# Value tiles between the first modulation's blocks, feature tiles made quarter by quarter, two modulation blocks in fp32

## The chip, the cores and the metric

The kernel runs on one core of a Trainium2 chip. The metric is the device time of one execution in microseconds. The reference is one step of a diffusion backbone with one layer: 128 context tokens and 512 latent tokens (640 together), width 2048, 8 neighbourhood heads and 8 latent-attention heads, a feed-forward width of 5632, all in float32.

## The reference, cut to what matters

```python
mod = silu(cond) @ w_mod + b_mod          # (2, 6*2048): a row for context, one for latent tokens
sh1, sc1, g1, sh2, sc2, g2 = split(mod, 6)
h = x * (1 + sc1) + sh1                   # needs the first two of the six parts, for all 2048 features
z = h @ w_in                              # q, k, v of the neighbourhood heads, then the latent projections
o = concat(neighbourhood_attention(...), latent_attention(...)) @ w_o
x = layernorm(alpha * x + g1 * o)
x = layernorm(alpha * x + g2 * swiglu(x * (1 + sc2) + sh2))
```

The change touches the first three steps: the shift and scale of the first modulation, h, and the columns of w_in that give the values v of the neighbourhood heads.

## The kernel before, in words

Matrix products run on TensorE in a split form: a float32 operand is cut into a high part (a copy rounded to fp32r, made by ScalarE) and a low part (the difference, made by VectorE), and a product is high x high, high x low and low x high. So every weight block of 128 x 1024 floats (512 KB) goes through DMA, one ScalarE instruction (`mod_split` or `split`, lines 917 and 904), one VectorE instruction (lines 1394 and 1343) and then TensorE. The counters `hi_ready`, `lo_ready` and `used` tell the next engine how many blocks, over all kinds, are through; each engine's program is written out in a fixed order.

The first modulation has 64 blocks, 8 for each of 8 units of 512 columns (0 to 3 shift, 4 to 7 scale), taken in order. They land in a ring of eight buffers `mraw`, loaded by the SP queue as soon as the low part of the block eight back is made. High and low parts have four buffers each. TensorE (`mod_block`) multiplies the two conditioning rows, as a stationary operand of 4 columns, with 512 moving columns, four matmuls a block; the result of a unit is 4 x 512 in one PSUM bank. ScalarE copies it to `modrow` (line 928), and TensorE turns the rows to columns (`turn_rows`, line 2020, four small fp32 matmuls) in bank 6. When all eight units are turned, VectorE adds the bias for all features at once (`mod1`, lines 1409 and 1410).

Then h is made, 16 feature tiles of 128 x 640: VectorE scales and shifts x into `pb` (line 1419, two instructions), ScalarE copies it to the high part `hh` (line 945), VectorE subtracts to get the low part `hl` (line 1424). Tiles 0 to 5 come with value block 0, then two with each block up to 5. x is loaded behind the last modulation block, alternating with the first four value blocks.

The value stage has 16 weight blocks: two halves of 512 output columns, 8 blocks of two feature tiles each. A block serves five token tiles of 128 (`tok_block`, lines 1942 to 1944), in PSUM banks 0, 1, 2, 3 and 7; a tile is six matmuls of 512 columns. The weights' parts have two buffers, so the split of block b + 2 waits for block b. Beside these blocks VectorE computes 16 blocks of the other modulation parts by multiply-add over the weights (`gemv`, line 1371), as many in each value block as `V_MODS` says: one in blocks 4 to 11, two in 12 to 15. Their partial sums are added on TensorE (`row_sums`, lines 1953 and 1954, fp32). Then come the neighbourhood blocks, the attention, the latent projections, w_o and the feed-forward part. POOL prepares bias tables from the moment the last unit is turned (line 709) and loads further constants into x's place when all of h is made (line 719).

Of the kernel before, what the change touches and what calls it, by code (L numbers as in the profile page):

```python
# [14 lines left out]
P = 128  # L15
# [41 lines left out]
V_MODS = [0] * 4 + [1] * 8 + [2] * 4  # L57
# [12 lines left out]

def stream_order():

    order = [("w", n) for n in range(B_V + 2)]
    m = 0
    for b in range(16):
# [23 lines left out]
POS = {x: p for p, x in enumerate(ORDER)}  # L99
MOD_SEQ = [x for k, x in ORDER if k == "m"]  # L100
# [13 lines left out]
def stream_row(p):  # L114

    kind, n = ORDER[p]
# [53 lines left out]
def build(nc, wstream, xT, xtok, cond, bmod, rpb, kcT, vc, ckvcT, krcT, lncol, lnrow, latg, bcol, rope, cap, ident, sel,  # L170
# [14 lines left out]
    with ctx:  # L185
# [37 lines left out]
        nq.close()  # L223
        qh = sb("qh", [P, T], f32r, att)
        kh = sb("kh", [P, KEYS], f32r, att)
        vh = sb("vh", [P, 6, P], f32, att)
        pb = sb("pb", [P, 3, T], f32, att)
        PT = sb("PT", [P, 5, LAT], f32, att)
# [7 lines left out]
        mraw = sb("mraw", [P, 8, 1024], f32, s0)  # L236
        mhi = sb("mhi", [P, 4, 1024], f32r, s0)
        mlo = sb("mlo", [P, 4, 1024], f32r, s0)
        modrow = sb("modrow", [4, 2, 512], f32, s0)
        selt = sb("selt", [5, 2 + 2 * P], f32, s0)  # L240
# [74 lines left out]
        xstage = acc[:, :].rearrange("p (k t) -> p k t", k=KD)  # L315
        vall = acc[:, 0:6 * NH * P].rearrange("p (k d) -> p k d", k=6)
# [184 lines left out]
        def slot_of(kind, n):  # L501
            return POS[(kind, n)] % 4

        def in_count(kind, n):

            return 16 * ((POS[(kind, n)] - B_V) // 4 + 1)
# [66 lines left out]
        MOD_BANKS = [7, 5]  # L573
# [23 lines left out]
        def _(sp):  # L597
            for n in range(8):
                sp.dma_start(mraw[:, n, :], wstream[n]).then_inc(mod_loaded[n], 16)
            with sp.Fori(1, B_V // 8) as i:  # L600
                for s in range(8):

                    sp.wait_ge(lo_ready, i * 8 + (s - 7))
                    sp.dma_start(mraw[:, s, :], wstream[i * 8 + s]).then_inc(mod_loaded[s], 16)

            for g in range(8):
                sp.dma_start(xstage[:, 2 * g:2 * g + 2, :], xT[:, 2 * g:2 * g + 2, :]).then_inc(x_in[g], 16)
                if g < 4:
                    sp.dma_start(raw[:, g, :], wstream[stream_row(B_V + g)]).then_inc(loaded[g], 16)

            def stream_load(p):

                sp.wait_ge(lo_ready, p - 3)
                sp.dma_start(raw[:, p % 4, :], wstream[stream_row(p)]).then_inc(loaded[p % 4], 16)

            for p in range(B_V + 4, len(ORDER)):
                stream_load(p)

            def gu_load(i, jj):
                for q in range(4):  # L620
                    if i is None and jj == 0:
                        sp.wait_ge(lo_ready, max(p for p in range(len(ORDER)) if p % 4 == q) + 1)
# [55 lines left out]
        def _(pool):  # L678
# [12 lines left out]

            for n in range(3):
                pool.memset(unit[:, n:n + 1], float(n == 1)).then_inc(unit_set, 1)
            pool.memset(PT[:, 1, 3 * P:4 * P], 0.0).then_inc(unit_set, 1)
# [10 lines left out]
            pool.wait_ge(mod1_psum, 8)  # L705
            for a in range(NH):
# [184 lines left out]
        def _(act):  # L891
# [6 lines left out]
            def split(i, n):  # L898

                act.wait_ge(loaded[slot_of("w", n)], at(i, 32, in_count("w", n)))  # L900
                if i is not None or n >= B_V + 2:

                    act.wait_ge(used, at(i, 4, n - 1))
# [7 lines left out]
            def mod_split(i, n):  # L911

                act.wait_ge(mod_loaded[n % 8], at(i, 32, 16 * (n // 8 + 1)))
                if i is not None or n >= 4:

                    act.wait_ge(used, at(i, 16, n - 3))
                nc.scalar.activation(mhi[:, n % 4, :], mraw[:, n % 8, :], ACT.Copy).then_inc(hi_ready, 1)

            def mod_pair(i, p):

                for b in range(16):
                    c = 2 * p + b // 8
                    if b % 8 == 7:

                        act.wait_ge(used, at(i, 16, 8 * c + 8))
                        if i is not None or c >= 2:
                            act.wait_ge(mod1_psum, at(i, 2, c - 1))
                        nc.scalar.activation(modrow[:, b // 8, :], ps[MOD_BANKS[b // 8]][0:4, :],
                                             ACT.Copy).then_inc(modrow_ready, 1)
                    n = 16 * p + b + 4  # L930
                    if i is not None or n < B_V:
                        mod_split(i, n)

            for n in range(4):
                mod_split(None, n)
            mod_pair(None, 0)
            with act.Fori(1, 3) as i:
                mod_pair(i, 0)
            mod_pair(None, 3)
            split(None, B_V)  # L940
# [6 lines left out]
            for b in range(16):  # L947
                if b < 6:
                    for k in (range(6) if b == 0 else range(2 * b + 4, 2 * b + 6)):
                        h_part(k)  # L950
                        if b == 0 and k == 1:
                            split(None, B_V + 1)
# [383 lines left out]
        def _(dve):  # L1336
# [3 lines left out]
            def split(i, n):  # L1340

                dve.wait_ge(hi_ready, at(i, 4, n + 1))
# [49 lines left out]
            def mod_split(i, n):  # L1392
                dve.wait_ge(hi_ready, at(i, 16, n + 1))
                V.tensor_tensor(mlo[:, n % 4, :], mraw[:, n % 8, :], mhi[:, n % 4, :].bitcast(f32),
                                ALU.subtract).then_inc(lo_ready, 1)

            for n in range(16):
                mod_split(None, n)
            with dve.Fori(1, 4) as i:
                for n in range(16):  # L1400
                    mod_split(i, n)
            split(None, B_V)

            dve.wait_ge(mod1_psum, 8)
            dve.wait_ge(consts_in, 16 * CONSTS)
# [3 lines left out]
            V.tensor_tensor(mod1[:, 0:KD, :], psum1[:, 0:KD, :], bc[:, 0:KD, :], ALU.add)  # L1409
            own.link(V.scalar_tensor_tensor(out=mod1[:, KD:2 * KD, :], in0=psum1[:, KD:2 * KD, :], scalar=1.0,  # L1410
                                            in1=bc[:, KD:2 * KD, :], op0=ALU.add, op1=ALU.add))

            def h_part(k):
                dve.wait_ge(x_in[k // 2], 16)
                if k >= 3:
# [10 lines left out]
            for b in range(16):  # L1426
                if b < 6:
                    ks = list(range(6) if b == 0 else range(2 * b + 4, 2 * b + 6))
                    if b == 0:
                        h_part(0)  # L1430
                    for k in ks:
                        if k + 1 < KD:
                            h_part(k + 1)
                        h_rest(k)
                        if b == 0 and k == 1:
                            split(None, B_V + 1)
# [500 lines left out]
        def _(pe):  # L1937
# [60 lines left out]
            def mod_block(i, n, b, chunk_free, bank, hi, lo):  # L1998

                pe.wait_ge(lo_ready, at(i, 16, n + 1))  # L2000
                if b == 0 and chunk_free is not None:

                    pe.wait_ge(modrow_ready, chunk_free)
                for kk in range(2):
                    w = slice(kk * 512, (kk + 1) * 512)
                    mm(ps[bank][0:4, :], condw[:, 2 * b + kk, :], hi[:, w], start=(b == 0 and kk == 0), stop=False)
                    ins = mm(ps[bank][0:4, :], condw[:, 2 * b + kk, :], lo[:, w], start=False, stop=(b == 7 and kk == 1))
# [5 lines left out]
            def turn_rows(i, c):  # L2013
                if i is None:
                    pe.wait_ge(consts_in, 16 * CONSTS)

                pe.wait_ge(modrow_ready, at(i, 2, c + 1))
                for j in range(4):
                    o = at(i, 16, 8 * c + 2 * j)
                    ins = mm(ps[6][:, bass.ds(o, 2)], modrow[:, c % 2, j * P:(j + 1) * P], selt[0:4, 0:2],  # L2020
                             start=True, stop=True)
                ins.then_inc(mod1_psum, 1)

            def mod_pair(i):
                for b in range(16):
                    c = b // 8
                    mod_block(i, b, b % 8, None if i is None else i * 2 + c - 1, MOD_BANKS[c],
                              mhi[:, b % 4, :], mlo[:, b % 4, :])
                    if b % 8 == 2 and (i is not None or c):
                        turn_rows(i, c - 1)  # L2030

            mod_pair(None)
            with pe.Fori(1, 4) as i:
                mod_pair(i)
            turn_rows(None, 7)

            for c in range(2):
                for b in range(8):
# [574 lines left out]
```

## Time and profile before

| | us |
|---|---|
| median of 3 runs | 2899.25 |
| lowest, highest | 2896.92, 2899.45 |
| profiled execution | 2901.91 |
| its span | 2900.4 |
| TensorE busy in it | 2817.4 (97%) |
| VectorE busy | 1890.2 (65%) |
| ScalarE busy | 1043.8 (36%) |
| DMA, mean rate | 131 GB/s |

The span runs from the first to the last recorded instruction of the profiled execution. Busy shares are averages over the whole span; the first 220 us, to which the change belongs, look otherwise and are shown by stretches further down. PE is TensorE, DVE VectorE, ACT ScalarE, PEld the weight loads of TensorE.

### The profile page before, as it was taken

What the parts mean: (1) busy time and instruction counts of PE and PEld (TensorE: products, weight loads), DVE (VectorE), ACT (ScalarE), POOL (GpSimd) and SP (SyncE); (2) the same over time, 40 slices, a digit from 0 to 9 for tenths busy, and PEclk for the clock granted to TensorE, in tenths of its full rate; (3) what the DMA queues carried; (4) which work ended last, traced back from release to release, by engine and by line L of the source; (5) the groups of instructions that cost most, each with busy time, mean ns of one, the idle gap of its engine ahead of it and who ended that gap; (6) DMA issues with size and microseconds to landing.
All of it is one profiled execution on the core that took longest, in us unless ns stands there. A gap on an engine that the chain in (4) does not pass through costs nothing.

```text
span 2900.4 us, 42090 instructions
## 1 busy us (share of the span) xinstructions
PE 2817.4 (97%) x15844; PEld 2497.6 (86%) x15844; DVE 1890.2 (65%) x2939; ACT 1043.8 (36%) x1813; POOL 184.6 (6%) x259
## 2 busy tenths in 40 slices
PE   7899999999999999899999999999999999999996
PEld 2679999887888777799999999999999888888885
DVE  8766666585885787866666666666666555424337
ACT  7422333224453212744444444444444312112121
POOL 1121111000001000000000000000000000000005
PEclk9999999999999999799999999999999999999998
DMA  9654333351335454122222222222222534223231
GB/s 382 273 185 155 127 128 128 122 190 57 114 113 222 157 173 172 71 111 101 100 100 96 100 100 100 99 93 95 100 100 100 198 122 172 79 93 133 80 124 73
DMA packets 104568, 379.82 MB, mean 131 GB/s; under 512 B 14014, under 2 KB 14418, under 8 KB 102426
## 3 DMA queue, kind: packets, MB, share of 16 engines
q1 hardware_dynamic: 89088, 317.36, 30.4%
q0 software_dynamic: 14800, 61.06, 5.8%
q8 instruction: 62, 1.02, 0.1%
q14 instruction: 32, 0.26, 0.0%
q10 hardware_dynamic: 586, 0.12, 0.0%
HBM read 346.97 MB, written 33.48 MB: 131 GB/s over the span
## 4 chain that ended last, share of the span: by engine, by line
PE 90%; DVE 5%; DMA 3%; ACT 2%; issue 1%; SPq 0%; ACTq 0%; DVEq 0%
PE ps L1942 15%; PE ps L1944 15%; PE ps L1943 15%; PE ps L2442 12%; PE ps L2441 12%; PE ps L2443 12%; DMA mraw<-in_wstream 2%; PE ps L2141 1%; PE ps L2106 1%; DVE ps L1870 1%; PE ps L2089 1%; DVE acc L1872 1%; DVE stat L1920 0%; DMA ostage<-oscr 0%; PE ps L2137 0%
## 5 line engine op out<-in xcount | busy, mean ns | idle before, releaser
L2441 PE MATMUL ps<-actl,ringh 128*128 128x320 f32 x1408 | 435.8, 310 | 2.8 <-DVE ringl L1741 2.8
L2443 PE MATMUL ps<-actl,ringl 128*128 128x320 f32 x1408 | 435.5, 309 | 0.0
L2442 PE MATMUL ps<-acth,ringh 128*128 128x320 f32 x1408 | 435.5, 309 | 0.0
L2441 PE MATMUL ps<-acth,ringh 128*128 128x320 f32 x1056 | 328.1, 311 | 7.6 <-DVE ringl L1741 7.6
L2442 PE MATMUL ps<-actl,ringh 128*128 128x320 f32 x1056 | 327.8, 310 | 0.0
L2443 PE MATMUL ps<-acth,ringl 128*128 128x320 f32 x1056 | 327.8, 310 | 0.0
L1942 PE MATMUL ps<-dwh,fring 128*128 128x512 f32 x820 | 319.5, 390 | 1.0 <-DVE dwl L1845 1.0
L1944 PE MATMUL ps<-dwh,fring 128*128 128x512 f32 x820 | 319.4, 390 | 0.0
L1943 PE MATMUL ps<-dwl,fring 128*128 128x512 f32 x820 | 319.4, 390 | 0.0
L1845 DVE TENSOR_TENSOR dwl<-raw,dwh 128x1024 fp32r<-128x1024 f32 x82 | 100.4, 1224 | 291.5 <-ACT dwh L1307 291.5
L1741 DVE TENSOR_TENSOR ringl<-raw,ringh 128x512 fp32r<-128x512 f32 x264 | 181.8, 690 | 163.0 <-ACT ringh L1241 163.0
L1343 DVE TENSOR_TENSOR wlo<-raw,whi 128x1024 fp32r<-128x1024 f32 x111 | 136.3, 1229 | 227.3 <-ACT whi L904 227.1
L1371 DVE SCALAR_TENSOR_TENSOR macc<-raw,conds,macc 128x512 f32<-128x512 f32 x390 | 269.7, 748 | 4.5 <-issue 1.2
L2441 PEld LDWEIGHTS ps<-actl,ringh 128*128 128x128 f32 x1408 | 264.4, 188 | 3.6 <-DVE ringl L1741 3.6
L2442 PEld LDWEIGHTS ps<-acth,ringh 128*128 128x128 f32 x1408 | 264.4, 188 | 0.0
L2443 PEld LDWEIGHTS ps<-actl,ringl 128*128 128x128 f32 x1408 | 264.4, 188 | 0.0
L1241 ACT ACTIVATE ringh<-raw 128x512 fp32r<-128x512 f32 x264 | 166.7, 632 | 264.4 <-PE ps L2443 264.4
L904 ACT ACTIVATE whi<-raw 128x1024 fp32r<-128x1024 f32 x111 | 117.4, 1058 | 381.6 <-PE ps L1944 381.6
L1307 ACT ACTIVATE dwh<-raw 128x1024 fp32r<-128x1024 f32 x82 | 86.9, 1060 | 414.9 <-PE ps L1944 410.1
L2441 PEld LDWEIGHTS ps<-acth,ringh 128*128 128x128 f32 x1056 | 199.4, 189 | 8.0 <-DVE ringl L1741 8.0
L2442 PEld LDWEIGHTS ps<-actl,ringh 128*128 128x128 f32 x1056 | 199.5, 189 | 0.0
L2443 PEld LDWEIGHTS ps<-acth,ringl 128*128 128x128 f32 x1056 | 199.4, 189 | 0.0
(309 smaller groups left out, 5777.4 us busy)
## 6 DMA issues: line engine op xcount, KB each, us to landing
raw<-in_wstream SPq DMA_DIRECT2D x503, 512.0 KB, 3.3
mraw<-in_wstream SPq DMA_DIRECT2D x64, 512.0 KB, 7.7
fscr<-fst POOLq DMA_DIRECT2D x44, 320.0 KB, 2.4
fst<-fscr SPq DMA_DIRECT2D x21, 640.0 KB, 4.1
acc<-in_xT SPq DMA_DIRECT2D x8, 640.0 KB, 16.0
oscr<-ost POOLq DMA_DIRECT2D x16, 320.0 KB, 2.5
ostage<-oscr POOLq DMA_DIRECT2D x16, 320.0 KB, 3.9
acc<-in_xtok POOLq DMA_DIRECT2D x1, 5120.0 KB, 18.2
```

Source lines behind the costliest of these rows:

```text
L904: nc.scalar.activation(hi_of(n), raw[:, slot_of("w", n), :], ACT.Copy).then_inc(hi_ready, 1)
L1241: nc.scalar.activation(ring(ringh, (HALF * j + h) % 4), gu_source(u, half), ACT.Copy).then_inc(ghi, 1)
L1343: V.tensor_tensor(lo_of(n), raw[:, slot_of("w", n), :], hi_of(n).bitcast(f32), ALU.subtract).then_inc(lo_ready, 1)
L1371: ins = V.scalar_tensor_tensor(out=v, in0=w, scalar=f, in1=v, op0=ALU.mult, op1=ALU.add)
L1741: V.tensor_tensor(ring(ringl, s), gu_source(u, half), ring(ringh, s).bitcast(f32), ALU.subtract).then_inc(glo, 1)
L1845: V.tensor_tensor(lo, raw[:, d % 4, :], hi.bitcast(f32), ALU.subtract).then_inc(dlo, 1)
L1942: mm(out, ah, bh, start=first, stop=False)
L1943: mm(out, ah, bl, start=False, stop=False)
L1944: return mm(out, al, bh, start=False, stop=last)
L2441: mm(out, ringh[:, s, w], ah, start=first, stop=False, skip_group_check=True)
L2442: mm(out, ringh[:, s, w], al, start=False, stop=False, skip_group_check=True)
L2443: ins = mm(out, ringl[:, s, w], ah, start=False, stop=last, skip_group_check=True)
```

## The change

The modulation's units are taken in the order 0, 4, 1, 5, 2, 6, 3, 7, so that each 16 blocks give shift and scale of one quarter of the features; `mod1` is then made in four parts, the first three in blocks 19, 35 and 51, the last behind block 63, and the quarter's four tiles of h follow it at blocks 0, 1, 5 and 6 counted from there. Value blocks 0 to 4 are done tile by tile between modulation blocks, from block 22 on, five tiles in eight blocks; value block 5 follows behind block 63, around the last turn of rows. Their splits stand at blocks 20, 27, 35, 43, 51 and 58. Loads of x and of the first eight value blocks stand between those of the modulation. Blocks 20 and 21 are not split: TensorE takes them from `mraw` in fp32, two matmuls each, with the stationary operand `condz` (conditioning rows and zeros). The ring `mraw` has six buffers instead of eight, high and low parts three instead of four, `modrow` one instead of two; part of them lies in the memory of later tiles. `V_MODS` puts the 16 gemv blocks into value blocks 7 to 15. Loops over blocks are written out.

```diff
-V_MODS = [0] * 4 + [1] * 8 + [2] * 4
+V_MODS = [0] * 7 + [1] + [2] * 7 + [1]
+UNITS = [0, 4, 1, 5, 2, 6, 3, 7]
+DIRECT = [20, 21]
+SPLIT = [j for j in range(B_V) if j not in DIRECT]
+X_LOAD = {6: 0, 9: 1, 22: 2, 25: 3, 38: 4, 41: 5, 54: 6, 57: 7}
+V_LOAD = {11: 0, 17: 1, 27: 2, 33: 3, 43: 4, 49: 5, 55: 6, 60: 7}
+V_SPLIT = {20: 0, 27: 1, 35: 2, 43: 3, 51: 4, 58: 5}
+V_TILES = {22 + 8 * v + x: (v, t) for v in range(5) for t, x in enumerate((0, 1, 3, 5, 6))}
+H_AT = {0: 0, 1: 1, 5: 2, 6: 3}
...
         def _(sp):
+            def mod_load(j):
+                if j - 6 in DIRECT:
+                    sp.wait_ge(used, used_count(mod_row(j - 6)))
+                elif j >= 6:
+                    sp.wait_ge(lo_ready, POS[("w", mod_row(j - 6))] + 1)
+                sp.dma_start(mraw[:, j % 6, :], wstream[mod_row(j)]).then_inc(mod_loaded[j % 6], 16)
+            for j in range(B_V):
+                mod_load(j)
+                if j in X_LOAD:
+                    g = X_LOAD[j]
+                    sp.dma_start(xstage[:, 2 * g:2 * g + 2, :], xT[:, 2 * g:2 * g + 2, :]).then_inc(x_in[g], 16)
+                if j in V_LOAD:
+                    stream_load(B_V + V_LOAD[j])
...
         def _(act):
+            def mod_split(j):
+                x = SPLIT.index(j)
+                act.wait_ge(mod_loaded[j % 6], 16 * (j // 6 + 1))
+                if x >= 3:
+                    act.wait_ge(used, used_count(mod_row(SPLIT[x - 3])))
+                nc.scalar.activation(mhi[:, x % 3, :], mraw[:, j % 6, :], ACT.Copy).then_inc(hi_ready, 1)
+            for j in range(B_V):
+                if j not in DIRECT:
+                    mod_split(j)
+                if j % 8 == 2 and j >= 8:
+                    mod_rows(j // 8 - 1)
+                if j in V_SPLIT:
+                    split(None, B_V + V_SPLIT[j])
+                q, x = divmod(j - 19, 16)
+                if 0 <= q < 3 and x in H_AT:
+                    h_part(4 * q + H_AT[x])
+            mod_rows(7)
+            split(None, B_V + 6)
+            for k in range(12, KD):
+                h_part(k)
+            split(None, B_V + 7)
...
         def _(dve):
+            dve.wait_ge(unit_set, 1)
+            V.tensor_copy(condz[:, :, 0:2], conds[:, 1])
+            for j in range(B_V):
+                if j not in DIRECT:
+                    mod_split(j)
+                if j in V_SPLIT:
+                    split(None, B_V + V_SPLIT[j])
+                q, x = divmod(j - 19, 16)
+                if 0 <= q < 3:
+                    if x == 0:
+                        mod1_part(q)
+                    if x in H_AT:
+                        h_part(4 * q + H_AT[x])
+                    if x - 1 in H_AT:
+                        h_rest(4 * q + H_AT[x - 1])
+            mod1_part(3)
+            h_part(12)
+            for k in range(12, KD):
+                if k + 1 < KD:
+                    h_part(k + 1)
+                h_rest(k)
+            split(None, B_V + 6)
+            split(None, B_V + 7)
...
         def _(pe):
+                    if j in DIRECT:
+                        ins = mm(ps[bank][0:4, :], condz[:, 2 * b + kk, :], mraw[:, j % 6, w], start=False, stop=False)
...
+            for j in range(B_V):
+                mod_block(j)
+                if j % 8 == 2 and j >= 8:
+                    turn_rows(j // 8 - 1)
+                if j in V_TILES:
+                    v, t = V_TILES[j]
+                    v_tiles(v, t, t + 1)
+            v_tiles(5, 0, 1)
+            turn_rows(7)
+            v_tiles(5, 1, TT)
             for c in range(2):
-                for b in range(8):
+                for b in range(6 if c == 0 else 0, 8):
```

`v_tiles(v, first, end)` waits for the block's low part and for h_ready of 2v + 2 tiles, and runs `tok_block` for the token tiles from `first` to `end`.

## Rows read from the trace of the kernel before

**Rows 1.** The chain that ended last, by engine.

```profile
PE 90%; DVE 5%; DMA 3%; ACT 2%; issue 1%; SPq 0%; ACTq 0%; DVEq 0%
```

**Rows 2.** Stretches: us, busy us of each engine (instructions), granted clock, DMA share, GB/s.

```profile
11.00:84.00 73.00, 63.53 (x269) 20.78 (x267) 66.54 (x55) 60.34 (x61) 0.42 (x1) 1.00 1.03 402
...
93.00:100.00 7.00, 1.05 (x9) 1.02 (x9) 5.34 (x12) 4.58 (x6) 4.70 (x8) 0.73 1.03 409
100.00:103.10 3.10, 3.10 (x8) 2.43 (x9) 3.10 (x7) 0.74 (x1) 0.50 (x1) 0.50 1.04 398
103.10:216.00 112.90, 112.90 (x482) 89.53 (x481) 72.71 (x107) 29.82 (x37) 24.14 (x42) 1.00 0.53 183
```

**Rows 3.** Timeline of ScalarE: start, duration, instruction, idle before and its releaser.

```profile
192.72 1.06 ACT L904 ACTIVATE whi<-raw 128x1024 fp32r<-128x1024 f32 x1 [5.94 <-PE ps L1944]
199.72 1.06 ACT L904 ACTIVATE whi<-raw 128x1024 fp32r<-128x1024 f32 x1 [5.94 <-PE ps L1944]
208.73 1.06 ACT L904 ACTIVATE whi<-raw 128x1024 fp32r<-128x1024 f32 x1 [7.96 <-PE ps L1944]
...
215.66 0.60 ACT L961 ACTIVATE acc<-ps 128x512 f32<-128x512 f32 x1 [0.80 <-PE ps L1944]
```

**Rows 4.** Timeline of TensorE around one turn of rows.

```profile
34.56 0.39 PE L2007 MATMUL ps<-mlo,condw 128*4 128x512 f32 x1
...
35.86 0.39 PE L2006 MATMUL ps<-mhi,condw 128*4 128x512 f32 x1
...
36.78 0.39 PE L2006 MATMUL ps<-mhi,condw 128*4 128x512 f32 x1
```

**Rows 5.** Timeline of ScalarE in the modulation; the last row is block 62.

```profile
31.49 1.06 ACT L917 ACTIVATE mhi<-mraw 128x1024 fp32r<-128x1024 f32 x1 [0.22 <-DMA mraw<-in_wstream]
32.45 0.57 ACT L928 ACTIVATE modrow<-ps 4x512 f32<-4x512 f32 x1
...
88.21 1.06 ACT L917 ACTIVATE mhi<-mraw 128x1024 fp32r<-128x1024 f32 x1 [0.22 <-DMA mraw<-in_wstream]
```

**Rows 6.** Timeline of all engines between the last modulation block and the value stage.

```profile
93.70 1.02 PE L2020 MATMUL ps<-selt,modrow 4*128 4x2 f32 x8 [0.77 <-ACT modrow L928]
...
95.67 0.18 DVE L1409 TENSOR_TENSOR mod<-ps,bcols 128x32 f32<-128x32 f32 x1
...
95.99 1.51 DVE L1419 TENSOR_SCALAR pb<-acc,mod 128x512 f32<-128x512 f32 x4
96.83 1.45 ACT L945 ACTIVATE hh<-pb 128x640 fp32r<-128x640 f32 x2 [2.33 <-DVE pb L1419]
...
99.97 0.77 PE L1942 MATMUL ps<-whi,hh 128*128 128x512 f32 x1 [5.25 <-issue]
```

**Rows 7.** Timeline of VectorE in the value stage.

```profile
100.92 0.80 DVE L1419 TENSOR_SCALAR pb<-acc,mod 128x512 f32<-128x512 f32 x2
101.63 0.82 DVE L1424 TENSOR_TENSOR hl<-pb,hh 128x640 fp32r<-128x640 f32 x1
102.37 0.80 DVE L1419 TENSOR_SCALAR pb<-acc,mod 128x512 f32<-128x512 f32 x2
...
200.81 1.23 DVE L1343 TENSOR_TENSOR wlo<-raw,whi 128x1024 fp32r<-128x1024 f32 x1 [0.81 <-ACT whi L904]
201.95 5.58 DVE L1371 SCALAR_TENSOR_TENSOR macc<-raw,conds,macc 128x512 f32<-128x512 f32 x8
```

**Rows 8.** DMA issues of the span: count, KB each, median us from issue to landing.

```profile
raw<-in_wstream SPq DMA_DIRECT2D x503, 512.0 KB, 3.3
mraw<-in_wstream SPq DMA_DIRECT2D x64, 512.0 KB, 7.7
```

**Rows 9.** Timeline of TensorE: one fp32 matmul of the row sums, in two records.

```profile
199.55 1.02 PE L1953 MATMUL ps<-macc,unit 128*2 128x512 f32 x2
```

**Rows 10.** Timeline of POOL: first load behind h, and the first bias table.

```profile
143.79 0.58 POOL L719 DMA_DIRECT2D acc<-in_vc  x1 [34.46 <-DVE hl L1424]
...
164.75 3.39 POOL L738 TENSOR_TENSOR acc<-acc 128x256 f32<-128x256 f32 x3 [2.69 <-DMA acc<-near]
```

More of the change, by code:

```diff
@@ L68, in lat_mods, with mod_row, pe_order, used_count @@
     return [24 + 2 * (b - 8) + x for x in range(2)] if b < 12 else [64 + 2 * (b - 12) + x for x in range(2)]
-def stream_order():
-    order = [("w", n) for n in range(B_V + 2)]
+UNITS = [0, 4, 1, 5, 2, 6, 3, 7]
[6 more added lines that the diff above has]
+H_AT = {0: 0, 1: 1, 5: 2, 6: 3}
+def mod_row(j):
+    return 8 * UNITS[j // 8] + j % 8
+def pe_order():
+    order = []
+    for j in range(B_V):
+        order.append(mod_row(j))
+        if j in V_TILES and V_TILES[j][1] == 4:
+            order.append(B_V + V_TILES[j][0])
+    return order
+PE_ORDER = pe_order()
+def used_count(n):
+    return PE_ORDER.index(n) + 1 if n in PE_ORDER else n + 1
+def stream_order():
+    order = []
+    for j in range(B_V):
+        if j not in DIRECT:
+            order.append(("w", mod_row(j)))
+        if j in V_SPLIT:
+            order.append(("w", B_V + V_SPLIT[j]))
+    order += [("w", B_V + v) for v in range(6, 8)]
     m = 0
-    for b in range(16):
+    for b in range(6, 16):
         order.append(("w", B_V + b + 2))
@@ L99 @@
 POS = {x: p for p, x in enumerate(ORDER)}
+SPLITS = [n for k, n in ORDER if k == "w"]
+RAWS = [(k, n) for k, n in ORDER if k == "m" or n >= B_V]
+RAW_POS = {x: B_V + p for p, x in enumerate(RAWS)}
+RAW_END = B_V + len(RAWS)
 MOD_SEQ = [x for k, x in ORDER if k == "m"]
@@ L114, in stream_row @@
 def stream_row(p):
-    kind, n = ORDER[p]
+    kind, n = RAWS[p - B_V]
     if kind == "m":
@@ L597, in _ @@
         def _(sp):
[L598 to L609, printed above, removed]
+            def mod_load(j):
[4 more added lines that the diff above has]
+                sp.dma_start(mraw[:, j % 6, :], wstream[mod_row(j)]).then_inc(mod_loaded[j % 6], 16)
             def stream_load(p):
-                sp.wait_ge(lo_ready, p - 3)
+                if p >= B_V + 4:
+                    sp.wait_ge(lo_ready, POS[RAWS[p - 4 - B_V]] + 1)
                 sp.dma_start(raw[:, p % 4, :], wstream[stream_row(p)]).then_inc(loaded[p % 4], 16)
-            for p in range(B_V + 4, len(ORDER)):
+            for j in range(B_V):
[5 more added lines that the diff above has]
+                    stream_load(B_V + V_LOAD[j])
+            for p in range(B_V + 8, RAW_END):
                 stream_load(p)
@@ L621, in gu_load @@
                     if i is None and jj == 0:
-                        sp.wait_ge(lo_ready, max(p for p in range(len(ORDER)) if p % 4 == q) + 1)
+                        sp.wait_ge(lo_ready, max(POS[x] for x in RAWS if RAW_POS[x] % 4 == q) + 1)
                     elif q == 0:
@@ L705, in _ @@
             pool.wait_ge(mod1_psum, 8)
+            pool.memset(PT[:, 1, 3 * P:4 * P], 0.0).then_inc(unit_set, 1)
             for a in range(NH):
@@ L908, in _, with mod_rows @@
             nc.scalar.activation(conds[:, 0], condf[:, :, :], ACT.Exp, scale=-1.0).then_inc(cond_exp, 1)
[L911 to L940, printed above, removed]
+            def mod_split(j):
[4 more added lines that the diff above has]
+                nc.scalar.activation(mhi[:, x % 3, :], mraw[:, j % 6, :], ACT.Copy).then_inc(hi_ready, 1)
+            def mod_rows(c):
+                act.wait_ge(used, used_count(mod_row(8 * c + 7)))
+                if c:
+                    act.wait_ge(mod1_psum, c)
+                nc.scalar.activation(modrow[:, :], ps[MOD_BANKS[c % 2]][0:4, :], ACT.Copy).then_inc(modrow_ready, 1)
             def h_part(k):
@@ L945, in h_part @@
                 nc.scalar.activation(hh[:, k, :], pb[:, k % 3, :], ACT.Copy).then_inc(h_hi, 1)
[L947 to L952, printed above, removed]
+            for j in range(B_V):
[13 more added lines that the diff above has]
+            split(None, B_V + 7)
+            for b in range(6, 16):
                 if b % 8 == 7:
@@ L1388, in _, with mod_split @@
             own.link(V.tensor_copy(condw[:, :, 0:2], conds[:, 1]))
+            dve.wait_ge(unit_set, 1)
+            V.tensor_copy(condz[:, :, 0:2], conds[:, 1])
             V.tensor_tensor(condw[:, :, 2:4], conds[:, 1], condw[:, :, 0:2].bitcast(f32),
                             ALU.subtract).then_inc(cond_ready, 1)
-            def mod_split(i, n):
-                dve.wait_ge(hi_ready, at(i, 16, n + 1))
-                V.tensor_tensor(mlo[:, n % 4, :], mraw[:, n % 8, :], mhi[:, n % 4, :].bitcast(f32),
+            def mod_split(j):
+                x = SPLIT.index(j)
+                dve.wait_ge(hi_ready, SPLITS.index(mod_row(j)) + 1)
+                V.tensor_tensor(mlo[x % 3], mraw[:, j % 6, :], mhi[:, x % 3, :].bitcast(f32),
                                 ALU.subtract).then_inc(lo_ready, 1)
[L1397 to L1405, printed above, removed]
             psum1 = ps[6][:, 0:4 * KD].rearrange("p (k c) -> p k c", c=2)
@@ L1408, in _, with mod1_part @@
             bc2 = bcols2[:, :].unsqueeze(2).to_broadcast([P, 2 * KD, 2])
-            V.tensor_tensor(mod1[:, 0:KD, :], psum1[:, 0:KD, :], bc[:, 0:KD, :], ALU.add)
-            own.link(V.scalar_tensor_tensor(out=mod1[:, KD:2 * KD, :], in0=psum1[:, KD:2 * KD, :], scalar=1.0,
-                                            in1=bc[:, KD:2 * KD, :], op0=ALU.add, op1=ALU.add))
+            def mod1_part(q):
+                dve.wait_ge(mod1_psum, 2 * q + 2)
+                if q == 0:
+                    dve.wait_ge(consts_in, 16 * CONSTS)
+                k = slice(4 * q, 4 * q + 4)
+                V.tensor_tensor(mod1[:, k, :], psum1[:, k, :], bc[:, k, :], ALU.add)
+                k = slice(KD + 4 * q, KD + 4 * q + 4)
+                V.scalar_tensor_tensor(out=mod1[:, k, :], in0=psum1[:, k, :], scalar=1.0, in1=bc[:, k, :],
+                                       op0=ALU.add, op1=ALU.add).then_inc(mod1_ready, 1)
             def h_part(k):
                 dve.wait_ge(x_in[k // 2], 16)
+                if k % 4 == 0:
+                    dve.wait_ge(mod1_ready, k // 4 + 1)
                 if k >= 3:
@@ L1424, in h_rest @@
                 V.tensor_tensor(hl[:, k, :], pb[:, k % 3, :], hh[:, k, :].bitcast(f32), ALU.subtract).then_inc(h_ready, 1)
[L1426 to L1436, printed above, removed]
+            for j in range(B_V):
+                if j not in DIRECT:
+                    mod_split(j)
+                if j in V_SPLIT:
+                    split(None, B_V + V_SPLIT[j])
[15 more added lines that the diff above has]
+            split(None, B_V + 7)
+            for b in range(6, 16):
                 split(None, B_V + b + 2)
@@ L1996, in feat_block, with mod_block @@
                 return ins
[L1998 to L2003, printed above, removed]
+            def mod_block(j):
+                c, b = divmod(j, 8)
+                bank = MOD_BANKS[c % 2]
+                if b == 0 and c >= 2:
+                    pe.wait_ge(modrow_ready, c - 1)
+                if j in DIRECT:
+                    pe.wait_ge(mod_loaded[j % 6], 16 * (j // 6 + 1))
+                else:
+                    pe.wait_ge(lo_ready, POS[("w", mod_row(j))] + 1)
@@ L2004, in mod_block @@
                 for kk in range(2):
                     w = slice(kk * 512, (kk + 1) * 512)
[L2006 to L2007 removed]
+                    if j in DIRECT:
+                        ins = mm(ps[bank][0:4, :], condz[:, 2 * b + kk, :], mraw[:, j % 6, w], start=False, stop=False)
+                    else:
+                        x = SPLIT.index(j) % 3
+                        mm(ps[bank][0:4, :], condw[:, 2 * b + kk, :], mhi[:, x, w], start=(b == 0 and kk == 0), stop=False)
+                        ins = mm(ps[bank][0:4, :], condw[:, 2 * b + kk, :], mlo[x][:, w], start=False,
+                                 stop=(b == 7 and kk == 1))
@@ L2022, in turn_rows @@
                 ins.then_inc(mod1_psum, 1)
[L2024 to L2034, printed above, removed]
@@ L2035, in _, with v_tiles @@
-            turn_rows(None, 7)
+            def v_tiles(v, first, end):
+                n = B_V + v
+                if first == 0:
+                    arrived(None, n)
+                    pe.wait_ge(h_ready, 2 * v + 2)
+                ins = tok_block(n, hh, hl, 2 * v, v == 0, False, TOK_BANKS[first:end], tile=range(first, end))
+                if end == TT:
+                    ins.then_inc(used, 1)
+            for j in range(B_V):
+                mod_block(j)
[4 more added lines that the diff above has]
+                    v_tiles(v, t, t + 1)
```

47 lines of the change are left out of this document (26 added, 21 removed).

## The prediction

> **What bounds the kernel now.** The chain that ended last is read first [rows 1]: TensorE holds 90% of it, so the kernel ends as much later or earlier as TensorE passes from the value blocks to the neighbourhood blocks. Then the table of stretches [rows 2]. From 11 to 84 us the DMA share is 1.03: a modulation ("mod") block of 512 KB comes every 1.28 us, while TensorE needs 0.93 us for its four matmuls, so there is room beside it. From 93 to 100 us TensorE is nearly empty, then it runs 3.1 us at a granted clock of 0.50, then 113 us without a gap. The change moves 30 of the 80 value tiles out of that full stretch into the stretch with room. But there VectorE is busy 66.5 of 73 us and ScalarE 60.3 [rows 2]: the question is whether these two deliver what both kinds of work need. The end of the value stage in this trace is the moment at which its last block is used, 215.66 us [rows 3].
>
> **Prices.** TensorE: a mod block 0.93 us (35.86 to 36.78); a turn of rows 1.07 us (the last matmul before it starts at 34.56, hands on 0.23 later, and the next block starts at 35.86) [rows 4]. A value block is 7.00 us from one release to the next (192.72 to 199.72), so a tile is 1.40 us; the row sums make it 9.0, so they add 2.0 [rows 3]. ScalarE: a high part of a weight block ends after 1.06 us and lets an instruction that stands ready start after 0.96; a row copy is 0.57 [rows 5]; the copy that makes hh 0.74, or 0.71 back to back [rows 6]. VectorE: scaling a feature tile ends after 0.80 us and hands on after 0.71; the low part hl takes 0.74; a low part of a weight ends after 1.23 and hands on after 1.14 [rows 7]; the two additions that make mod1 take 0.32 (95.67 to 95.99) [rows 6]. Handing over costs 0.02 us from ScalarE to VectorE and about 0.05 between the others, read off the gap of 95.99 + 0.80 to 96.83 [rows 6] and the like.
>
> **Blocks 0 to 21.** These stay bound by DMA. Block 62 lands at about 88.1, ahead of its high part [rows 5], so block n lands at 88.1 - 1.28 x (62 - n); up to block 18 the new order puts two x loads (640 KB, 1.6 us each) and two value loads (1.28 us each) ahead, so it lands at 31.8 + 5.8 = 37.6 us. A ring of six buffers instead of eight costs nothing as long as a load lands within 6 x 1.28 less 2.5 us for splitting, 5.2 us: the 7.7 us of now [rows 8] are six loads waiting for each other, and a load of the later stream lands in 3.3 [rows 8]. The other end, 7.7 us kept with six buffers, would be (7.7 + 2.5) / 6 = 1.7 us a block and 8 to 9 us late at block 21; I take nothing. Splits, block 18 and its turn end at 41.8. Then VectorE makes mod1 (0.32 us), tile 0 of h, the value block's low part, tile 1, two rests, and ScalarE's copies stand between: the high part of block 22 starts at 47.5, block 22 on TensorE at 49.8. The two blocks in fp32 save VectorE and ScalarE a split each. Their price isn't in the trace; the nearest are the row sums, fp32 matmuls of 512 columns, two records each, 1.02 us at most for the pair [rows 9]; a block has two such matmuls, so 1.8 to 2.0 us instead of 0.93. They end at 46.3, inside the time that TensorE waits for block 22: cost nothing (1.1 us each if that cover were gone). The extra copy and memset at the start (0.2 us) lie before DMA has filled the ring: nothing.
>
> **TensorE's work from block 22.** 42 mod blocks x 0.93 = 39.1; 30 tiles x 1.40 = 42.0; 6 turns x 1.07 = 6.4; ten value blocks x 7.0 = 70.0; row sums 2.0. Sum 159.5 us: from 49.8 it would end at 209.3 if it never waited.
>
> **What it waits for.** The new order on ScalarE is: high part of block j, then the copy of h tile k, and only then the high part of j + 1. The copy waits for VectorE's scaling, which in blocks 19, 35 and 51 waits for the turn that TensorE does behind blocks 18, 34, 50. From the end of turn(34): 0.1 + mod1 0.32 + scaling 0.80 + 0.05 + copy 0.71 + high part 1.06 + 0.02 + low part 1.23 + 0.05 = 4.3 us until block 36 may start; TensorE has block 35 and one tile, 2.33. It waits 2.0. Queued behind the waiting copy on ScalarE is every later high part, though its data landed long before. Block 37 hangs on the second copy: low part 1.14, scaling 0.80, 0.05, 0.71, 1.06, 0.02 = 3.8 us from one low part to the next, against 2.33: 1.4 us. Block 38: low part and rest of h on VectorE 1.87 against 0.93: 0.9. Blocks 39 and 40 catch up; blocks 41 and 42 repeat it, 0.4 and 1.4 us. A quarter costs 2.0 + 1.4 + 0.9 + 0.4 + 1.4 = 6.2 us. For the quarter at 51 the fifth value block's split falls on block 58, into the same knot: 1.4 more, 7.6. In the first quarter TensorE is already idle for tiles 0 and 1; blocks 25 and 26 wait 0.4 and 1.4. Behind block 63 the last quarter: from the last turn 0.4 for mod1, 6.15 for four h tiles (pitch 1.45, 100.92 to 102.37 [rows 7]), 1.28 for the sixth block's low part, which stands behind them: 7.85 against four tiles of 5.6, 2.2 us. Waits: 1.8 + 6.2 + 7.6 + 2.2 = 17.8 us. The last mod block ends at about 145 us.
>
> The Trainium skill, "TensorE: Matmul & The Clock Gate", section "Architectural detail", says that ScalarE and VectorE are strict first-in first-out. By that rule the waits stand and the sum is 2911; an engine that passed a waiting copy would give the first rival's 2893. The trace can't decide it, since nowhere now does a ready instruction stand behind an unready one long enough.
>
> **Sum.** 209.3 + 17.8 + 0.17 (a matmul of 0.40 us is released that much behind the start of the next, 0.23) = 227.3, against 215.7: 11.6 us later. What follows is bound by TensorE and moves with it. Gemvs: with two a block VectorE needs 1.14 + 8 x 0.69 = 6.7 of 7.0 us [rows 7], so seven such blocks still fit. POOL's tables wait for the last turn (94.7 us now [rows 6], about 148 then) and for the last h tile (143.8, then about 154), and need 24 us from there [rows 10]; they are wanted behind 228: nothing. The profiled execution took 2901.91 us (span 2900.4), and by the sum 2913.5; the median of the runs is 2899.25, 2.7 lower, so the forecast is 2911.
>
> **The rivals.**
> *TensorE never waits from block 22 (the other side).* High and low parts are three blocks deep, so VectorE could be far enough ahead to hide each round trip. For it: between knots VectorE's 1.14 a block is faster than TensorE's 1.88 mean. Against: two blocks ahead are worth 2.3 to 3.3 us and the round trip 4.3. Its place is blocks 36 to 42 and 52 to 58; 209.3 + 0.17 against 215.7 gives -6.2: 2893. It decides as soon as the waits sum to under 6.2 us instead of 17.8.
> *Half of the waits.* Only the first wait of each pair stays, the rest is caught up: 1.0 + 3 + 3.5 + 2 = 9.5 us in all, +3.3: 2902 to 2903.
> *The clock falls too.* TensorE sits idle before block 22 for 3.5 us; now a gap of 5.3 us ahead of 99.97 [rows 6] is followed by 3.1 us at 0.50, the 1.2 GHz level [rows 2], in which 8 matmul records begin where 3.1 / 0.233 would make 13: 5 x 0.233 = 1.2 us. Gaps of 0.35 us before every mod block (1.28 less 0.93) leave it at 1.00 [rows 2], and what 2 us do no row shows. Once costs 1.2 us, in each of five knots 6 to 7: 2918.
> The Trainium skill, same page, section "Why this matters for your kernels", warns of idle gaps between bursts of matmuls; the trace agrees for the one gap above, with its 3.1 us at 0.50. [...]
>
> **How the numbers follow.** Forecast 0.65 (by itself 2905 to 2916), clock 0.12, half of the waits 0.13, no waits 0.10. The range 2899 to 2919 leaves out the rival without waits and a tail on each side. What a measurement of this kernel can tell from no change is 0.2%, 5.8 us: 2893.5 to 2905. Slower takes the forecast, the clock and little of the half: 0.76. The same takes most of the half and some of the other two: 0.17. Faster 0.07.
>
> **What would show it.** Block 22 on TensorE at 50 us; idle TensorE before mod blocks put down to VectorE's low part, some 14 us between 50 and 145, in clusters of 6 to 8 us behind blocks 34 and 50; on ScalarE the h copy waiting for VectorE directly ahead of a high part; the last mod block at 145 and the last value block released at 227; granted clock 1.00 from 52 us. Low parts of 36 and 52 ready when TensorE wants them would make it wrong, as would block 22 far from 50.

## The result, and the profile after

| | median us | lowest, highest | runs |
|---|---|---|---|
| before | 2898.14 | 2896.63, 2901.01 | 7 |
| changed | 2910.55 | 2909.51, 2911.69 | 7 |

The ratio is 1.004, with a 95% interval of 1.003 to 1.005: the change costs 12.4 us. The profiled execution of the changed kernel took 2910.55 us, span 2909.0.

In the changed kernel line 975 is the high part of a modulation block, 1451 its low part, 2085 and 2086 its four matmuls, 2012 to 2014 the six of a value tile, 2082 those of an fp32 block, 2100 the turn of rows, 987 the h copy, 1477 its scaling, 1482 hl, 961 and 1396 the parts of a value block. (Two of the three low buffers lie in hh's memory, so low parts are named mlo or hh.) First ScalarE's timeline: the end of the value stage.

```profile
221.37 1.06 ACT L961 ACTIVATE whi<-raw 128x1024 fp32r<-128x1024 f32 x1 [7.96 <-PE ps L2014]
...
228.30 0.60 ACT L1014 ACTIVATE acc<-ps 128x512 f32<-128x512 f32 x1 [0.80 <-PE ps L2014]
```

The last row answers to 215.66 in [rows 3]: the stage ends 12.6 us later in these two executions, and the medians differ by 12.4. Now the stretches of the changed kernel, columns as in [rows 2].

```profile
19.00:50.00 31.00, 21.39 (x79) 6.37 (x78) 22.02 (x24) 19.44 (x21) 0.00 (x0) 0.93 1.02 410
49.70:53.00 3.30, 3.27 (x9) 1.93 (x10) 2.96 (x4) 0.92 (x2) 0.00 (x0) 0.53 1.03 407
53.00:76.00 23.00, 22.80 (x102) 13.04 (x101) 17.23 (x17) 15.02 (x17) 0.00 (x0) 1.00 0.82 299
86.70:90.40 3.70, 3.69 (x10) 2.37 (x11) 2.94 (x4) 1.10 (x3) 0.00 (x0) 0.54 1.00 388
103.00:145.00 42.00, 35.56 (x157) 19.93 (x156) 28.64 (x33) 22.34 (x26) 0.00 (x0) 1.00 0.71 252
155.50:159.00 3.50, 3.50 (x10) 2.72 (x10) 0.02 (x1) 0.00 (x0) 3.50 (x7) 0.56 0.93 304
```

Up to 50 us DMA is full, with six buffers too (share 1.02). From 50 on it mostly isn't (0.82 and 0.71 in the longer stretches), VectorE has a quarter to a third of its time free (busy 17.2 of 23 us and 28.6 of 42), and from 76 us on TensorE has gaps all the same. The timeline of TensorE gives them: each row is the first matmul of a mod block or of a value block, or a turn; in brackets the idle time before it.

```profile
49.73 0.59 PE L2085 MATMUL ps<-mhi,condw 128*4 128x512 f32 x1 [3.36 <-DVE hh L1451]
...
53.43 0.39 PE L2085 MATMUL ps<-mhi,condw 128*4 128x512 f32 x1
...
59.39 0.39 PE L2085 MATMUL ps<-mhi,condw 128*4 128x512 f32 x1 [0.20 <-DVE mlo L1451]
...
75.56 0.40 PE L2086 MATMUL ps<-hh,condw 128*4 128x512 f32 x1
75.89 1.05 PE L2100 MATMUL ps<-selt,modrow 4*128 4x2 f32 x8
76.87 0.40 PE L2085 MATMUL ps<-mhi,condw 128*4 128x512 f32 x1
...
81.14 0.39 PE L2085 MATMUL ps<-mhi,condw 128*4 128x512 f32 x1 [1.79 <-DVE hh L1451]
...
84.84 0.39 PE L2085 MATMUL ps<-mhi,condw 128*4 128x512 f32 x1 [1.21 <-DVE hh L1451]
...
86.71 0.44 PE L2085 MATMUL ps<-mhi,condw 128*4 128x512 f32 x1 [0.79 <-DVE mlo L1451]
...
90.58 0.40 PE L2085 MATMUL ps<-mhi,condw 128*4 128x512 f32 x1
...
118.14 0.40 PE L2085 MATMUL ps<-mhi,condw 128*4 128x512 f32 x1 [1.77 <-DVE hh L1451]
...
121.83 0.40 PE L2085 MATMUL ps<-mhi,condw 128*4 128x512 f32 x1 [1.21 <-DVE mlo L1451]
...
123.70 0.39 PE L2085 MATMUL ps<-mhi,condw 128*4 128x512 f32 x1 [0.78 <-DVE hh L1451]
...
129.67 0.40 PE L2085 MATMUL ps<-mhi,condw 128*4 128x512 f32 x1 [0.24 <-DVE hh L1451]
...
133.36 0.40 PE L2085 MATMUL ps<-mhi,condw 128*4 128x512 f32 x1 [1.22 <-DVE hh L1451]
...
136.65 0.39 PE L2085 MATMUL ps<-mhi,condw 128*4 128x512 f32 x1 [1.22 <-DVE mlo L1451]
...
154.44 0.50 PE L2012 MATMUL ps<-whi,hh 128*128 128x512 f32 x1 [1.99 <-DVE wlo L1396]
...
163.09 0.40 PE L2012 MATMUL ps<-whi,hh 128*128 128x512 f32 x1
```

The rows with a wait are blocks 22; 26; 36, 37, 38; 52, 53, 54; 57, 58 and 59; and value block 6. The rows at 53.43 and 90.58 are blocks 23 and 39, at 163.09 value block 7: they show how long the block and the tiles ahead of them took. The idle time is counted from the modelled end of a matmul, 0.17 us behind the moment at which the next could start, so a row of 1.79 is a loss of 1.95 us (block 35, which starts at 76.87, and its tile are through 2.33 us later, at 79.19, and block 36 starts at 81.14). What stands between is seen on the other two engines, in order of time, around block 36 (the turn behind block 34 ends at 76.9):

```profile
77.31 0.80 DVE L1477 TENSOR_SCALAR pb<-acc,mod 128x512 f32<-128x512 f32 x2
...
78.14 0.74 ACT L987 ACTIVATE hh<-pb 128x640 fp32r<-128x640 f32 x1 [3.34 <-DVE pb L1477]
...
78.79 1.04 ACT L975 ACTIVATE mhi<-mraw 128x1024 fp32r<-128x1024 f32 x1
...
79.86 1.23 DVE L1451 TENSOR_TENSOR hh<-mraw,mhi 128x1024 fp32r<-128x1024 f32 x1 [1.75 <-ACT mhi L975]
81.01 0.80 DVE L1477 TENSOR_SCALAR pb<-acc,mod 128x512 f32<-128x512 f32 x2
```

ScalarE stands idle for 3.34 us at the h copy, with the high part of block 36 behind it; VectorE then waits 1.75 us for that high part. Both have time and neither can use it.

### The profile page after: what moved, and what is told of

Same layout as the page of the kernel before. It is cut to its first block, busy times and chain, and to the rows that moved or that the text cites. A ratio compares the mean times of both kernels' runs of the same rounds, so it can differ in the third digit from the quotient of the medians.

```text
span 2909.0 us, 41766 instructions
## 1 busy us (share of the span) xinstructions
PE 2818.4 (97%) x15844; PEld 2497.6 (86%) x15844; DVE 1887.2 (65%) x2944; ACT 1039.1 (36%) x1811; POOL 185.7 (6%) x260
## 3 DMA queue, kind: packets, MB, share of 16 engines
q8 instruction: 63, 1.03, 0.1%
## 4 chain that ended last, share of the span: by engine, by line
PE 88%; DVE 5%; ACT 1%; DMA 1%; issue 0%; ACTq 0%; DVEq 0%
PE ps L2012 15%; PE ps L2014 15%; PE ps L2013 15%; PE ps L2526 12%; PE ps L2528 12%; PE ps L2527 12%; PE ps L2226 1%; PE ps L2191 1%; DVE ps L1940 1%; PE ps L2174 1%; DVE acc L1942 1%; DVE stat L1990 0%; PE ps L2222 0%; DMA ostage<-oscr 0%; ACT stagef L1261 0%
```

## The experiments

Each was timed in turn with the kernel before on the same chip, and the ratio is to it; the changed kernel stands at 1.004. There were two sets: copy_later, copy_later_v6, all_split and tiles_behind, in which the kernel before has a median of 2900.04 us, and more_fp32, v6_first, rest_later and gemvs_later, in which it has 2901.26. Across sets, and against the changed kernel, times are best compared by their ratios. "Stage end" is, as above, the moment in the one profiled execution at which the last value tile is released.

**copy_later.** The order on ScalarE alone.

```diff
-                q, x = divmod(j - 19, 16)
+                q, x = divmod(j - 20, 16)
                 if 0 <= q < 3 and x in H_AT:
                     h_part(4 * q + H_AT[x])     # ScalarE: the copy, one block later
```

> The changed kernel with one edit: on ScalarE each h copy of the first three quarters stands one modulation block later, behind the next block's high part. Theory (the order on ScalarE makes the waits): block 22 starts on TensorE near 48 instead of 49.7 us, the waits at blocks 36, 37 and 52, 53 shrink from 1.9 and 1.4 to 0.1 and 0.3 us, those at 38 and 54 stay at 0.9, those at 57 to 59 go; the waits ahead of mod blocks from 50 to 145 fall from 12 to about 3 us. Value stage released near 214 instead of 228.3, time about 2896 to 2899. Rival (VectorE has no room, whatever the order): the waits move to other blocks, stage end above 225, time above 2907. Rival (the clock decides): the same waits go, but the time falls by no more than the falls of the clock that go with them, 3 us or less.

Measured: 2895.85 us, ratio 0.9989 (0.9978 to 0.9999). TensorE's gaps from 40 to 145 us, and the stage's end:

```profile
47.68 0.39 PE L2085 MATMUL ps<-mhi,condw 128*4 128x512 f32 x1 [1.52 <-DVE hh L1451]
...
79.96 0.40 PE L2085 MATMUL ps<-mhi,condw 128*4 128x512 f32 x1 [0.79 <-DVE mlo L1451]
...
112.30 0.40 PE L2085 MATMUL ps<-mhi,condw 128*4 128x512 f32 x1 [0.77 <-DVE hh L1451]
...
140.03 0.50 PE L2012 MATMUL ps<-whi,hh 128*128 128x512 f32 x1 [1.99 <-DVE wlo L1396]
...
212.33 0.60 ACT L1014 ACTIVATE acc<-ps 128x512 f32<-128x512 f32 x1 [0.80 <-PE ps L2014]
```

The same instructions in another order on one engine end the stage 16 us earlier, and the median is 14.7 us lower (forecast: a stage end near 214 and 2896 to 2899 us, so a little too long). The waits at 36, 37, 52, 53, 58 and 59 are gone; those at 38, at 54 and ahead of value block 6 are left. VectorE does all its work in that time, so it had room. DMA is nearer its own limit than before (share 0.90 to 1.03 in each stretch of 10 us from 50 to 120, for 0.66 to 0.98 in the changed kernel). The granted clock reads 1.00 in each stretch of 10 us from 40 to 180. A fall's price in the changed kernel is 1.4 to 1.65 us (below), three of them 4.6, so the clock can't be the 16 us. Take the time from the start of block 22 to the stage end, less 159.5 us of work and 0.17 for the release: TensorE loses 18.9 us in the changed kernel (49.73 to 228.30) and 5.0 us here (47.68 to 212.33). The other 2 us are the earlier start of block 22.

**more_fp32.** The order stays, and the high parts behind the copies go.

```diff
-DIRECT = [20, 21]
+DIRECT = [20, 21, 36, 37, 52, 53]
```

> The changed kernel with blocks 36, 37, 52 and 53 in fp32 too, in the order as it is: four more blocks cost TensorE 0.9 us each, but no high part stands behind the waiting h copies. Theory (TensorE waits for the high parts that are queued behind the copies): the waits of 1.9, 1.4 and 0.9 us at blocks 36 to 38 and 52 to 54 go, those at 57 to 59 too, because VectorE gets ahead; block 43 starts some 4 us and block 59 some 9 to 10 us earlier than in the changed kernel, the stage is released near 219 us, time 2899 to 2903. Rival (the TensorE work itself is what made the change slower): four fp32 blocks more, 3.7 us longer, 2914.

Measured: 2902.85 us, ratio 1.0005 (0.9996 to 1.0014), stage end 219.54. TensorE does 3.7 us more and is done 8.8 us earlier: what it waited for were the parts of the blocks queued behind the copies. Its time is within the forecast and the rival's 2914 is out. Of the waits from block 23 to 63 one is left, 0.57 us ahead of block 59. This edit takes four splits from ScalarE and VectorE as well as the queueing, so by itself it doesn't part order from amount of work; copy_later, which takes away no work, does. The turns show the gain (TensorE, behind blocks 34, 42, 50 and 58):

```profile
75.69 1.05 PE L2100 MATMUL ps<-selt,modrow 4*128 4x2 f32 x8
...
93.23 1.05 PE L2100 MATMUL ps<-selt,modrow 4*128 4x2 f32 x8
...
108.75 1.05 PE L2100 MATMUL ps<-selt,modrow 4*128 4x2 f32 x8
...
126.29 1.05 PE L2100 MATMUL ps<-selt,modrow 4*128 4x2 f32 x8
```

From turn to turn 17.5 us instead of 21.5 in the changed kernel (75.89 to 97.38), with the same 15.5 between 42 and 50.

**all_split.** `DIRECT = []`, nothing else.

> The changed kernel with blocks 20 and 21 split like the others (no fp32 blocks). Theory (VectorE and ScalarE are the bound there, the fp32 blocks lie in time that TensorE has idle): block 22 starts 3 us later, near 53, and the time is 1.5 to 3.5 us longer, 2912 to 2914. Rival (the fp32 blocks cost TensorE what they save the others): no change, 2910 to 2911.

Measured: 2916.51 us, ratio 1.0058 (1.0044 to 1.0072), stage end 233.02: 4.7 us later than in the changed kernel, and the median 6 us higher, so the two fp32 blocks were worth more than the 1.5 to 3.5 us expected, and not nothing. TensorE now waits 3.21 us ahead of block 20 and 2.96 ahead of block 21, and the clock falls behind each:

```profile
45.97 0.59 PE L2085 MATMUL ps<-mhi,condw 128*4 128x512 f32 x1 [3.21 <-DVE hh L1451]
...
50.79 0.59 PE L2085 MATMUL ps<-mhi,condw 128*4 128x512 f32 x1 [2.96 <-DVE mlo L1451]
...
52.66 0.59 PE L2085 MATMUL ps<-mhi,condw 128*4 128x512 f32 x1
```

Block 22 starts at 52.66, 2.9 us later, as expected. The other 1.8 us come behind it, where this execution also has a wait of 1.21 us and a fall of the clock ahead of 70 us (granted 0.83 from 60 to 70) that the changed kernel hasn't; I had counted the splits and not that.

**tiles_behind.** No value tiles among the modulation blocks; all 16 value blocks behind block 63.

```diff
-V_LOAD = {11: 0, 17: 1, 27: 2, 33: 3, 43: 4, 49: 5, 55: 6, 60: 7}
-V_SPLIT = {20: 0, 27: 1, 35: 2, 43: 3, 51: 4, 58: 5}
+V_LOAD = {11: 0, 17: 1, 27: 2, 33: 3, 43: 4, 49: 5}
+V_SPLIT = {20: 0, 27: 1}
-V_TILES = {22 + 8 * v + x: (v, t) for v in range(5) for t, x in enumerate((0, 1, 3, 5, 6))}
+V_TILES = {}
...
-            v_tiles(5, 0, 1)
             turn_rows(7)
-            v_tiles(5, 1, TT)
...
-                for b in range(6 if c == 0 else 0, 8):
+                for b in range(8):
```

> The changed kernel without value tiles among the modulation blocks: units in the new order, h by quarters, two fp32 blocks, loads of x and of value blocks between, but all 16 value blocks behind block 63. It shows what the tiles alone bring. Theory: the h copies and splits alone, with nothing of TensorE's to wait for, bring block 63 to an end near 125 us instead of 144; then 16 x 7.0 + 2 + 1 us: the stage is released near 240, time about 2922. Rival (the tiles are what costs, the rest is free): block 63 near 106 us, stage end near 221, time about 2904.

Measured: 2939.93 us, ratio 1.0136 (1.0120 to 1.0151). Both forecasts were too short: the last turn starts at 139.55 instead of about 125, the stage ends at 254.83.

```profile
50.00:139.00 89.00, 64.56 (x206) 21.47 (x204) 64.25 (x76) 49.29 (x56) 0.00 (x0) 0.73 0.75 268
```

Two of the longer waits, one behind the other:

```profile
78.02 0.59 PE L2080 MATMUL ps<-mhi,condw 128*4 128x512 f32 x1 [3.18 <-DVE hh L1448]
...
81.71 0.59 PE L2080 MATMUL ps<-mhi,condw 128*4 128x512 f32 x1 [1.82 <-DVE hh L1448]
```

The mean clock is 0.73: with longer gaps it falls again and again, and at the lower level a mod block takes 1.7 us (four matmuls 0.43 us apart in its trace), more than a split. The last turn of before starts at 93.70 [rows 6], so without the value tiles the modulation is 46 us longer; the h tiles, the loads that stand between, and the slow clock share that, and this run doesn't part them. The value tiles then bring 26.5 us of stage end (254.8 less 228.3) and 28 to 29 us of time, more than the 11.5 that I gave them (2922 less 2910.5). The clock is part of it: with them its mean is 0.96 from 49 to 145 us.

**v6_first.** The wait behind the last mod block alone.

```diff
                 h_rest(k)
-            split(None, B_V + 6)
+                if k == 13:
+                    split(None, B_V + 6)
             split(None, B_V + 7)
```

> The changed kernel with the low part of value block 6 made behind h tile 13 instead of behind tile 15, and nothing else. Theory: the wait of 2.2 us ahead of value block 6 goes and the clock's fall behind it too, stage end near 225, 3 to 3.5 us less than the changed kernel: 2907. Rival (the fall comes from the waits up to 137 us, not from this one): only 2 us less, and about 3 us at a clock near 0.5 somewhere behind 140.

Measured: 2909.62 us, ratio 1.0026 (1.0016 to 1.0037), stage end 226.18. The stage end is 2.1 us earlier, the size that the rival gives. The times don't decide: the median is 0.9 us below the changed kernel's, the ratio 0.14% (4 us), and the intervals meet. The wait is gone, and the clock falls elsewhere, somewhat ahead of the 140 us of the rival:

```profile
118.00:133.00 15.00, 11.58 (x49) 6.14 (x47) 11.01 (x15) 9.67 (x12) 0.00 (x0) 1.00 0.81 283
133.00:136.00 3.00, 1.96 (x13) 1.28 (x11) 3.00 (x4) 2.60 (x3) 0.00 (x0) 0.74 0.38 115
136.00:139.50 3.50, 3.50 (x9) 2.11 (x10) 2.66 (x3) 1.06 (x1) 0.00 (x0) 0.50 0.17 68
```

That execution has no fall behind the waits at 36 to 38 and has one behind those at 58 and 59; the changed kernel's has it the other way round. Nor is the rival's reason shown, that the fall behind value block 6 comes from the earlier waits: in more_fp32 those at 36 to 38 and 52 to 54 are gone, and the clock still falls there (granted 0.66 from 145 to 150). What brings a fall at a wait of this size stays open; each kernel was profiled once.

The trace shows one thing more. With the clock up behind 38, blocks 41 and 42 wait:

```profile
91.95 0.40 PE L2086 MATMUL ps<-mhi,condw 128*4 128x512 f32 x1 [0.21 <-DVE mlo L1451]
...
95.65 0.40 PE L2086 MATMUL ps<-mhi,condw 128*4 128x512 f32 x1 [1.20 <-DVE hh L1451]
```

**copy_later_v6.** Both edits together.

> As copy_later, and VectorE makes the low part of value block 6 behind h tile 13 instead of behind tile 15. Theory: the wait of 2.2 us ahead of value block 6 goes, and with it the clock's fall behind it (1.3 us), so 3 to 3.5 us less than copy_later: about 2893 to 2895, faster than before by 0.1 to 0.2%. Rival (that fall of the clock comes anyway): 2 us less only, with a granted clock near 0.5 for 3 us behind 140.

Measured: 2893.86 us, ratio 0.9981 (0.9972 to 0.9990), stage end 209.87, 2.5 us earlier than copy_later. The expected 3 to 3.5 us held a fall of the clock, and in copy_later the wait ahead of value block 6 had brought none.

**rest_later.** On top of it, `x - 2` for `x - 1` at `h_rest`.

> As copy_later_v6, and VectorE makes each hl one block later too, behind the next block's low part. Theory: the waits of 0.8 us that are left at blocks 38 and 54 go, 1.5 us less than copy_later_v6, stage end near 208.3; about 0.25% below the kernel before. Rival: TensorE then waits for hl at the value tiles of these blocks, nothing gained.

Measured: 2893.40 us, ratio 0.9967 (0.9955 to 0.9979), faster than the kernel before by 0.2 to 0.45% (six runs; the two medians alone give 0.9973). Stage end 208.11, 1.8 us earlier than copy_later_v6; the waits at 38 and 54 shrink from 0.78 to 0.30 and 0.32 us. That this last step makes the kernel faster than copy_later_v6 isn't shown by the times, whose intervals overlap.

**gemvs_later.** The kernel before with the new `V_MODS` alone.

> The kernel before with the new V_MODS alone: no gemv in value blocks 0 to 6, two in each of 8 to 14. Theory: VectorE has 7.0 us a block for 6.7 us of work, value stage released at 215.7 us as before, no change in time. Rival (two gemvs a block are too many): 1 to 2 us longer, with TensorE waiting for a low part behind block 13.

Measured: 2899.01 us, ratio 0.9995 (0.9986 to 1.0003): no change, and no wait of TensorE for a low part in the value stage. This part of the change is free as far as the times can tell; its stage end, in one execution, is 216.62 against 215.66.

## Why the prediction was right

*Forecast 2911, measured 2910.55.* Step by step, for the stage's end (227.3 forecast, 228.3 measured):

- *Block 22 at 49.8.* It starts at 49.73. DMA bounds what comes before (share 1.02 from 19 to 50 us), and the turn behind block 18 ends at 41.76, for 41.8, so the smaller ring costs nothing. My condition for that, a load landing within 5.2 us, was too strict: from 15 to 50 us the loads of the ring took 6.6 us in the median, and DMA stayed full. The fp32 blocks take 3.60 us for both and lie in idle time; without them the end comes 4.7 us later (all_split).
- *TensorE's work, 159.5 us.* It stands. A turn, priced as before, took 1.08 for 1.07 (76.87 less 75.56 and 0.23), and the sum at the end of this list closes with 159.5.
- *The waits at 36 to 38: 2.0, 1.4, 0.9.* Measured 1.95, 1.37 and 0.94 (81.14 less 79.19, 84.84 less 83.47, 86.71 less 85.77: what stands ahead is a block of 0.93, with a tile of 1.40 or without), and the same at 52 to 54. At 57, 58 and 59, 0.39, 1.36 and 1.29 for 0.4, 1.4 and 1.4. The mechanism was shown from two sides: with the copy one block later (copy_later) those at 36 and 37 go, and with nothing to split behind it (more_fp32) all three do.
- *The total of the waits, 17.8.* This term was too large: 0.4 + 4.5 + 7.3 + 2.2 = 14.3 us (7.3 from 52 to 59). Blocks 25, 26, 41 and 42 waited 0.6 us between them instead of 3.6 (0.37 at 26, 0.20 at 42), because the clock had fallen before them: while TensorE was slow, the low parts caught up. In v6_first, where it did not fall behind 38, blocks 41 and 42 lose 0.37 and 1.37 us. The terms of a quarter also add up to 6.1, not the 6.2 that stands there.
- *The clock at 1.00.* The third rival came in part. The granted clock was near 0.5 in three stretches, behind the 3.4 us ahead of block 22, behind the waits at 36 to 38 and behind the wait of value block 6. Each costs what the block it meets takes too long: 53.43 - 49.73 - 2.33 = 1.4, 90.58 - 86.71 - 2.33 = 1.5, and 163.09 - 154.44 - 7.00 = 1.65 us, 4.6 in all. The first two took the place of waits that would have come anyway: the second fall and block 42 cost 1.54 + 0.20 = 1.74 us, and without the fall, in v6_first, blocks 41 and 42 cost 0.37 + 1.37 = 1.74; the first fall and block 26 cost 1.37 + 0.37, where 1.8 was forecast. So only the last one is added to the end. I had priced a fall at 1.2 and added it in full. The Trainium skill, "TensorE: Matmul & The Clock Gate", section "Why this matters for your kernels", warns of long idle gaps between bursts of matmuls. The trace agrees for the gap of 3.4 us ahead of block 22, with 0.53 behind it. The shorter waits at 36 to 38 were followed by 0.54, and those at 52 to 54, equal to them, by 1.00.
- *The sum.* 49.73 + 159.5 + 14.3 + 4.6 + 0.17 = 228.3, as measured. Waits 3.5 less, clock 4.6 more: two errors that are for the most part one trade, and they nearly cancel. That the stage end came out within 1 us is partly this. That the time came out within 0.5 us is luck besides: the forecast stood on 2899.25 for the kernel before, which has 2898.14 in the new runs, so the difference was 11.8 forecast and 12.4 measured.
- *What follows moves with it.* By the medians, 12.4 for 12.6 us. The two profiled executions differ by only 8.6, because that of before loses time further on, in places that the change doesn't touch. Followed by the same instructions, the distance is 12.6 us at 502 us of the kernel before and 11.0 at 524, between which a slow stretch of the clock lies in both and is longer in before (0.87 from 500 to 540, against 0.91 in the changed kernel 12.6 us later). It is 10.9 at 935 and 7.8 at 955: there before waits 1.5 us longer for a load of the attention's output (7.58 against 6.04 us) and has a fall of the clock behind it (0.91 from 940 to 960), which the changed kernel hasn't (1.00).

*The rival of the other side* (TensorE never waits, 2893) had the right price and the wrong condition: the depth of three blocks doesn't hide the round trip in the order of the changed kernel, but another order does, and copy_later_v6 and rest_later reach it (stage end 209.9 and 208.1, for 209.5). Whether more than three buffers would hide it in the old order wasn't run. The Trainium skill, same page, section "Architectural detail", has ScalarE and VectorE strictly first-in first-out; the trace now agrees, with 3.34 us of ScalarE idle at a copy ahead of a high part that could have been made. *Half of the waits* (2902 to 2903) didn't come: no wait was halved, some were taken over by the slow clock.

## What to carry to other kernels

Busy shares said that VectorE and ScalarE had room, and they had; what decided was a chain through both of them that stood in front of ready work in their queues. When work that hangs on a late result is put between the blocks of a stream, let each engine take the next block's part before the dependent piece, and compare the length of the dependent chain (4.3 us here) with the work that the engine it feeds, TensorE here, still has in stock (2.33 us). And where a slow stretch of the clock comes just ahead of a wait, count them once: here the slow stretch took the place of the wait (1.74 us either way).

## What the runs showed that I had not expected

- Equal groups of waits (1.95, 1.37, 0.94 us) were followed once by 3.4 us at half clock and once by none, and in v6_first neither group was followed by one. A wait of 2.16 us alone ahead of value block 6 was followed by a fall in the changed kernel and in more_fp32, and by none in copy_later and all_split.
- Without value tiles, with gaps of up to 3.2 us, the mean clock is 0.73 over 89 us, and the modulation takes 46 us longer instead of the 32 that were expected.
